# Two small steps of a two-model transformer kernel move: a remainder later in VectorE's order, another from GpSimd to VectorE

## The reference

```python
z = u @ w_in
qa, ka, va, cq, ckv, kr, gl = jnp.split(z, SPLIT_POINTS, axis=-1)
qa = apply_axial_rope(rmsnorm(qa, q_norm_g), cos_a, sin_a)         # 8 heads of 64
ka = apply_axial_rope(rmsnorm(ka, k_norm_g), cos_a, sin_a)
ya = blocked_attention(qa, ka, va, 1.0 / math.sqrt(GQA_HEAD_DIM))
qb = (rmsnorm(cq, q_a_norm_g) @ w_q_up).reshape(b, s, MLA_HEADS, MLA_QK_DIM)   # 8 heads of 64 + 32
q_nope, q_rope = qb[..., :MLA_NOPE_DIM], qb[..., MLA_NOPE_DIM:]
q_rope = apply_axial_rope(q_rope, cos_b, sin_b)
kvb = (rmsnorm(ckv, kv_a_norm_g) @ w_kv_up).reshape(...)
yb = blocked_attention(qb, kb, vb, 1.0 / math.sqrt(MLA_QK_DIM))
```

## Time and profile before

| | before |
|---|---|
| median of 3 runs | 2993.22 us (2992.01 to 2995.95) |
| the profiled execution | 2993.22 us, span 2991.4 us |
| PE busy | 2829.0 us, 95% |
| DVE busy | 1614.9 us, 54% |
| ACT busy | 1147.8 us, 38% |
| POOL busy | 748.1 us, 25% |
| mean granted TensorE clock | 0.972 |

### The profile page before, as it was taken

The page is one execution under the profiler, slowest core; times in us unless marked ns, Lnnn a source line. Parts: engine busy times, 40 slices in busy tenths (PEclk is TensorE's granted clock), DMA queues, the critical chain, the costliest instruction groups (busy, mean ns, idle before and its releaser), DMA issues.

```text
span 2991.4 us, 33731 instructions
## 1 busy us (share of the span) xinstructions
PE 2829.0 (95%) x12862; PEld 2317.4 (77%) x12862; DVE 1614.9 (54%) x2065; ACT 1147.8 (38%) x1758; POOL 748.1 (25%) x607
## 2 busy tenths in 40 slices
PE   8899999999998999999999967999999999999997
PEld 6677887888776778788887766878887789878886
DVE  5786446334367854453434895455533558555533
ACT  5675334222346753332223343322322348422221
POOL 2563113213025621140223161022200014122200
PEclk9999999999999999999999888999999989999999
DMA  3011322233220112223332201222232210123332
GB/s 136 28 43 43 99 92 85 94 97 99 85 85 22 43 53 95 85 92 99 99 95 87 79 19 60 92 92 95 96 106 99 83 52 1 57 92 99 99 103 88
DMA packets 75634, 236.68 MB, mean 79 GB/s; under 512 B 9776, under 2 KB 18240, under 8 KB 75488
## 3 DMA queue, kind: packets, MB, share of 16 engines
q1 hardware_dynamic: 74288, 231.31, 23.9%
q0 software_dynamic: 928, 3.27, 0.3%
q10 hardware_dynamic: 272, 0.06, 0.0%
HBM read 228.31 MB, written 2.10 MB: 77 GB/s over the span
## 4 chain that ended last, share of the span: by engine, by line
PE 86%; DVE 8%; ACT 2%; issue 1%; POOL 1%; DMA 1%; SPq 1%; DVEq 0%; POOLq 0%; ACTq 0%
PE bank L1800 27%; PE bank L1802 27%; PE bank L1801 27%; PE bank L2097 2%; PE bank L1961 1%; DVE S5S L1668 1%; DMA RAWW<-weights 1%; DVE STAT L1494 1%; PE bank L2003 1%; DVE S5S L1659 1%; SPq L817 1%; DVE WL L1383 1%; ACT WH L1072 1%; PE bank L1903 0%; DVE PHL L1388 0%
## 5 line engine op out<-in xcount | busy, mean ns | idle before, releaser
L1383 DVE TENSOR_TENSOR WL<-RAWW,WH 128x1024 fp32r<-128x1024 f32 (+2 forms) x424 | 573.7, 1357 | 862.5 <-ACT WH L1072 862.4
L1800 PE MATMUL bank<-UH,WH 128*128 128x512 f32 (+1 forms) x1920 | 762.3, 397 | 53.7 <-DVE UL L1393 29.4
L1801 PE MATMUL bank<-UL,WH 128*128 128x512 f32 (+1 forms) x1920 | 754.5, 393 | 0.0
L1802 PE MATMUL bank<-UH,WL 128*128 128x512 f32 (+1 forms) x1920 | 754.0, 393 | 0.0
L1072 ACT ACTIVATE WH<-RAWW 128x1024 fp32r<-128x1024 f32 (+2 forms) x424 | 433.9, 1027 | 368.5 <-DMA RAWW<-weights 368.0
L1800 PEld LDWEIGHTS bank<-UH,WH 128*128 128x128 f32 (+1 forms) x1920 | 364.6, 190 | 141.6 <-issue 58.1
L1801 PEld LDWEIGHTS bank<-UL,WH 128*128 128x128 f32 (+1 forms) x1920 | 365.0, 190 | 78.2 <-issue 2.4
L1802 PEld LDWEIGHTS bank<-UH,WL 128*128 128x128 f32 (+1 forms) x1920 | 364.4, 190 | 77.6
L1800 PE MATMUL bank<-HH,WH 128*128 128x512 f32 x512 | 199.2, 389 | 0.0
L1801 PE MATMUL bank<-HL,WH 128*128 128x512 f32 x512 | 199.2, 389 | 0.0
L1802 PE MATMUL bank<-HH,WL 128*128 128x512 f32 x512 | 199.2, 389 | 0.0
(11 more groups left out here) (340 smaller groups left out, 4711.2 us busy)
## 6 DMA issues: line engine op xcount, KB each, us to landing
RAWW<-weights SPq DMA_DIRECT2D x424, 512.0 KB, 3.4
X<-x SPq DMA_DIRECT2D x8, 256.0 KB, 5.4
FF<-tables POOLq DMA_DIRECT2D x2, 1024.0 KB, 7.2
U<-S5U SPq DMA_DIRECT2D x16, 128.0 KB, 2.4
GEL<-U SPq DMA_DIRECT2D x128, 16.0 KB, 1.8
out<-FF SPq DMA_DIRECT2D x8, 256.0 KB, 2.0
S5B<-s_b POOLq DMA_DIRECT2D x1, 512.0 KB, 4.3
S5C<-s_c POOLq DMA_DIRECT2D x1, 512.0 KB, 4.3
```

The source lines that it names most:

```text
L1383: dve.tensor_tensor(slot_words(WL, c % SLOTS, size), slot_words(RAWW, c % SLOTS, size), f32(slot_words(WH, c % SLOTS, size)), ALU.subtract ...
L1800: nc.tensor.matmul(out_, w[0], x_[0], start=start, stop=False, **how)
L1801: nc.tensor.matmul(out_, w[0], x_[1], start=False, stop=False, **how)
L1802: return nc.tensor.matmul(out_, w[1], x_[0], start=False, stop=stop, **how)
```

## The change

One step moves in the list, and one step changes its engine and its arithmetic. `turn_low` for the heads of the second attention no longer stands beside `turn_out` but behind `att_out_lo` of the same x. The gain is no longer applied in `latent`: that becomes a plain multiply by the inverse root, `latent_high` applies the gain as the scale of its copy, and `latent_low` computes tile times gain minus high part on VectorE instead of tile minus high part on GpSimd.

```diff
@@ attention_steps
             plan.add("turn_out", **rotation)
-            plan.add("turn_low", **rotation)
         if x < n:
             plan.add("att_scores", "u", h=x // KT, t=x % KT)
...
         if 0 <= h < 2 * HEADS and phase == 3:
             plan.add("att_out_lo", h=h, pv=h)
+        if 1 <= m_out <= HEADS and out_phase == 1:
+            plan.add("turn_low", **rotation)
         latents(x)
@@ gpsimd
-                elif st.kind == "latent_low":
-                    k = st.i if st.what == "cq" else CQT + st.i
-                    pool.wait_ge(c_h.sem, c_h.after(l, st.cn))
-                    pool.tensor_tensor(CL[:, k, :], CF[:, k, :], f32(CH[:, k, :]), ALU.subtract).then_inc(c_l.sem, 1)
@@ scalar
                 elif kind == "latent_high":
-                    k, _ = small_input(l, st)
+                    k, gain = small_input(l, st)
                     act.wait_ge(c_n.sem, c_n.after(l, st.cn))
-                    act.activation(CH[:, k, :], CF[:, k, :], ACT.Copy).then_inc(c_h.sem, 1)
+                    act.activation(CH[:, k, :], CF[:, k, :], ACT.Copy, scale=gain).then_inc(c_h.sem, 1)
@@ vector
-                    dve.scalar_tensor_tensor(CF[:, k, :], CF[:, k, :], gain, (RCQ if st.what == "cq" else RKV)[:], ALU.mult, ALU.mult
-                                             ).then_inc(c_n.sem, 1)
+                    dve.tensor_tensor(CF[:, k, :], CF[:, k, :], (RCQ if st.what == "cq" else RKV)[:], ALU.mult).then_inc(c_n.sem, 1)
+                elif kind == "latent_low":
+                    k, gain = small_input(l, st)
+                    dve.wait_ge(c_h.sem, c_h.after(l, st.cn))
+                    dve.scalar_tensor_tensor(CL[:, k, :], CF[:, k, :], gain, f32(CH[:, k, :]), ALU.mult, ALU.subtract
+                                             ).then_inc(c_l.sem, 1)
```

## The result

The changed kernel takes 3016.01 us (median of 4 runs, 3014.45 to 3020.18) beside 2993.99 us before: ratio 1.0073, 95% interval 1.0060 to 1.0086. It is 22 us slower, 0.7%. The prediction had 3017 us.

A forecast was written before the change was run, and what follows sets the result against it. TensorE, busy in 95% of the span, was taken as the bound. The late `turn_low` +20.3, clock falls +6.7 and latents -3.0 gave +24.0 us on 2993.2, so 3017 us; range 3003 to 3035.

The forecast's parts named there:

- The chain behind the row maximum: VectorE, second attention: MQL ends 0.90 + 2.55 us after tile x's scores begin; TensorE starts 0.05 us later.
- The sum of part one: `turn_low` behind `att_out_lo`: seven heads in each layer shift TensorE by 1.12 to 1.64 us, in sum +20.3 us.
- The last head costs nothing: Eighth head of each layer: the three operations slip into VectorE's 2.17 us wait for MQH, at no cost.
- The clock: TensorE behind the new waits: four falls of the granted clock, +6.7 us; ends 0 and +23.5.
- Part two: Latents: ten operations go from GpSimd to VectorE; shorter holds win 0.6 and 0.85 us a layer, -3.0 us.
- The fall at each head: Rival: the clock falls at nearly every head, +40.8 us, 3034 us; chance 0.17.
- VectorE held more: Rival: each of the ten new VectorE operations is held or uncovered, +34.4 us, 3028 us; chance 0.10.
- broken bursts: Rival: without L880 GpSimd pauses and VectorE gets in, +8.9 us, 3002 us; chance 0.12.
- that of the other sign: Rival, faster: `turn_low` is in time if TensorE has 3.5 us of work between; -7.3 us, 2986 us; chance 0.04.

The follow-up runs named there:

- part one alone: Kernel before with only `turn_low` moved behind `att_out_lo`, the latents as before: 3015.61 us, 1.0070 of before.
- part two alone: Kernel before with only `latent_low` on VectorE and the gain moved, `turn_low` in its old place: 2993.12 us, 0.9996 of before.
- `mla_mm` in between: Changed kernel with the next head's `mla_mm` matmuls moved behind the score tile and transposes, ahead of the wait for MQL: 2986.02 us, 0.9972 of before.

## Why the prediction was right, by its steps

- **The chain behind the row maximum** was right, and it carried the result. Five places of `turn_low` and its neighbours follow it: TensorE waits 0, 0.50, 1.10, 1.64 and 1.76 us at a regular head (2.01 at every second one of the last), and the kernel is 0, 3, 6, 15 and 21 us over before. The forecast's "some 25 us in all" of waiting was 31.9: its own fourteen waits add up to 12 x 1.76 + 2 x 2.2 = 25.5 us, and the last heads' 4.3 us were not added to them.
- **The sum of part one**, 20.3 us. To measure it I compare the start of the same matmul before and after. From the last matmul in front of the first head's wait to the last in front of the last head's, the changed kernel loses 13.62 us in layer 0 and 13.50 in layer 1. Four falls of the clock are in it; each costs about 1.56 us, by the time from one head's first scores to the next with a fall and without (223.50 to 238.82, 15.32 us, beside 195.76 to 209.51, 13.75 us, both behind a wait of 2.01 us), 6.2 us in all. That leaves 20.9 us. The kernel with part one alone gives the same: 11.99 + 13.62 less 4.7 for three falls, 20.9 us. Missed were 0.09 us of the step from scores to values, and 0.25 us at the heads where an odd head's output stands in front of MQL; I took 2.55 us for all.
- **The last head costs nothing**: right (2.23 us of waiting against 2.14), but it had a side that I did not see: in the changed kernel and with part one alone the clock stayed up behind it.
- **The clock** was the term with the wrong size: +6.7 us forecast. Four falls came, as many as forecast, and cost 6.2 us. But the matmuls behind the two last heads' waits came 1.48 and 1.70 us earlier than before, since the falls there were gone: +3.0 us net. (With that head alone moved it was 1.55 us where the clock stayed up and 0.17 us where it fell.) I had priced the new falls and not asked about those already there. That the count was four is partly luck: part one alone had three. And the odds were not as I took them, 1/4 for each of twelve waits near 1.76 us: in the two kernels together seven of sixteen new waits of 2.01 to 2.45 us were followed by a fall, and none of twelve of 1.75 or 1.76 us.
- **Part two**, -3.0 us forecast, came nearly so where it acts. `latent_low` was to be held to 125.76 and was held to 126.30 in a run that stands 0.38 us later there, so to 125.92. TensorE's two idle times are 0.66 and 0.70 us shorter in layer 0, and 0.61 and 0.84 in layer 1 (3.89 and 2.81 before, 3.28 and 1.97 after). Over the two stretches (110 to 160 and 910 to 970 us of before) the same matmuls gain 2.5 us, in the changed kernel and with part two alone; with part one alone, whose latents are as before, they gain 0.5 us there too, so some 2.0 to 2.5 us are the part's. The runs can't tell this from nothing (1 us faster, interval from 4 faster to 1.5 slower).
- **The rivals.** The fall at each head, VectorE held more and broken bursts did not come. The sharpest one was that of the other sign: it named 3.5 us of TensorE's work as the point from which it decides, and with `mla_mm` in between it came true, with 8 us.

So the sum, 24.0 against 22.0 us (22.4 in the profiled spans), is close partly because errors of opposite sign met: 3.7 us too much for the clock, against 0.6 too little for part one, 0.5 too much gain from part two, and 1.0 us by which the profile after is longer in stretches that no edit touches.

## What to carry to other kernels

A step in an in-order list has two prices, for what waits behind it on its own engine and for what waits for its result; count both from the producer that the moved step now stands behind, not from the step itself. Where the consumer has other work that can stand in front of its wait, move that work too: the same edit cost 21 us without it and was worth 19 us with it. When a hold on an engine is made shorter, look at which operation is held next before counting the gain. When pricing falls of the clock behind new waits, count the falls that the old waits already cause and the change may end.

## What the runs showed of the hardware

- A VectorE operation with two tiles from memory was held through several GpSimd instructions in a row (3.59 us in the earlier trace rows) and in other cases until the end of the one running (1.16 us); it ended 0.54 to 0.57 us after GpSimd's last each time. Which of the two it will be I could not tell from the traces. GpSimd is held as well: its multiply of 1.04 us took 2.67 us before (130.20) and 3.28 us in the changed kernel (130.11), where VectorE runs two and three such operations in a row.
- Two VectorE operations whose tiles start at different partitions (64 and 0) start 0.70 to 0.73 us apart instead of 0.60. In "VectorE: DVE Perf Modes", Two Vector instructions with no wait between them, the Trainium skill says that an instruction whose operands start in another quadrant of partitions than the last one's is held until the earlier ones have finished; the trace fits: YBL ended at 222.72 and MQL started at 222.76, while at 208.78 MQL started before YBL had ended (208.85).
- The clock fell behind 7 of 16 new waits of 2.01 to 2.45 us (changed kernel and part one alone), and behind none of the 24 of 1.64 to 1.76 us (the same two, and `turn_low` behind `att_lo`). But length alone does not tell: waits of 2.13 to 2.24 us at the last head were followed by a fall in both layers before, in none of the changed kernel, and in one of two with that head alone moved.
